# Two-layer mixer and expert network on one core: the delta layer's beta and decay products with the weights standing

## The chip, the cores and the metric

The kernel runs on one core of a Trainium2 chip. The metric is the device time of one execution in microseconds. Engines are named as in the profile: PE is TensorE's matmul, PEld its weight load, DVE is VectorE, ACT ScalarE, POOL GpSimd, and SP the engine that issues most of the DMAs. Everything is in fp32. The program is one launch of 25,742 instructions.

## What is computed

A block of two layers with experts, then a second block of two layers, on 256 tokens of 1024 features. The change is in the odd layer of the first block, the gated delta rule. Cut to what matters:

```python
def gated_deltanet_mixer(h, w_in, conv_w, a_log, dt_bias, o_norm, w_out):
    proj = h @ w_in                                   # 256 tokens x (4096 + 16)
    qkv = silu(causal_dwconv(proj[..., :3072], conv_w))
    q, k, v = split(qkv)
    gate, b_raw, a_raw = split(proj[..., 3072:], (1024, 8, 8))
    q, k = l2norm(q), l2norm(k)
    beta = sigmoid(b_raw)                             # 8 heads
    g = -exp(a_log) * softplus(a_raw + dt_bias)       # 8 heads, the decay
    o = gated_delta_chunked(q, k, v, g, beta)
    return (gated_rmsnorm(o, gate, o_norm)) @ w_out
```

`b_raw` and `a_raw` are the last 16 columns of `h @ w_in`: a product of 256 tokens by 1024 features with 1024 by 16 weights. This is the product that is changed.

## The kernel before

Each engine has one program, written out in order: `res_*` (residual and layer norm), `delta_*` (the delta layer), `moe_*` (experts). Engines meet through counted semaphores: `P.up(...)` marks an event of PE, `V.up` of DVE, `C.up` of ACT, and `e.wait_ge(*on(...))` waits for one. Nothing reorders the work; each engine does its list from top to bottom.

`hT` holds the normed activations with the features on the partitions: eight groups `k` of 128 features, 256 tokens each. A `mm(out, lhsT, rhs)` (line 339 and 340) loads `lhsT` as the standing weights and streams `rhs`; each call in fp32 shows in the trace as two LDWEIGHTS and two MATMUL, so the counts of the trace are twice the calls. A row "128*32 128x256" is a product with standing weights of 128 partitions by 32 columns and 256 streamed columns.

The layer's projection goes in 16 units of 256 columns. Unit 0 is split: `first_unit_pe(e, 0, ...)` does its first 128 tokens between the two halves of the layer norm, with `hT` standing where the second half of the tokens isn't there yet, and the call in `delta_pe` (L1999) does `m = 1`, the other 128 tokens. Each of its four parts is four calls: parts 0 and 1 are output columns 0 to 127, parts 2 and 3 the others. Then `proj_t(e, ("d_ba",), 16, hT, ("d_bac",))` (L2000, the helper at L403) makes the beta and decay columns: for each half `m` of the tokens and each `k`, a 128x128 block of `hT` stands and the 16 columns of the weights stream: 16 calls. Its output lies with tokens on the partitions, in columns 0 to 15 and 256 to 271 of a PSUM bank.

Then PE goes on with `unit_pe(1)`, `unit_pe(2)` (32 calls in all, 256 columns streamed), `sums()` (running sums of the decay, which wait for DVE's event `d_g`), `differences(0)` and `(1)` (64x64 products of `d_gm`), and units 3 to 15, with sums of heads, turns and the sums for the modulation (`ada_sum_pe`, four products with 32 columns of weights into the four quarters of a bank, L589) between them.

DVE's list `delta_dve` begins with the wait for `d_ba` (L2278), copies the 32 columns out of the bank (L2279, event `d_bac`), and works out beta and the decay from them in about twenty small steps up to `d_g`, sixteen `masked` products (`d_gm`), and then the convolution units; after unit 0 of these it waits for `d_cum` 3, the last of PE's `sums()`. ACT's list `delta_act` begins with the wait for `d_bac` (L2182), and copies unit 0 out of its bank (`copy_in(0)`) only behind the exponentials of beta and decay. SP's list `delta_sp` loads unit 0, `d_ba` (64 KB), and then units 1 to 15 into a ring of four slots. A slot is loaded again when PE has used it (`P.also("used", ...)`). POOL loads the modulation's weights in the same way, each released by DVE. The table `tab` of small constants comes in one DMA at the start.

`rs_t` is a tile of 128 by 2 by 512 that holds gate rows for the expert layer before, and decay rows later in the delta layer.

Of the kernel before, what the change touches and what calls it, by code (L numbers as in the profile page):

```python
# [252 lines left out]
def build(nc, A, out, at, lo, tab_at):  # L253
    ctx = ExitStack()
    with ctx:
# [55 lines left out]
        conv_w, colv, hyf = F("conv"), F("cols"), F("hyf")  # L311
        rpe33, gkw2, poolw = F("rpe")[0:33, :], F("gkw2")[0:16, :], F("poolw", 2, 64)
        hw1, hw2, rtb, adt = F("hw1")[0:33, :], F("hw2")[0:64, :], F("rtb", 2, 64), F("adt", 2, 8)
        one_f, sel_f = F("one"), F("sel")
        ident, flip, ones = K("ident"), K("flip"), K("ones")
        eps5, eps6 = K("eps")[:, 0:1], K("eps")[:, 1:2]
        one_c = K("eps")[:, 2:3]
# [18 lines left out]
        def pair(v):  # L336
            return v.rearrange("p (m n) -> p m n", m=2)
# [1634 lines left out]
        def first_unit_pe(e, m, parts=(0, 1, 2, 3)):  # L1972

            u = unit(("d_proj", 0), 8, 256)
            if m == 0 and 0 in parts:
                fill_bank(e, ("d_proj", 0), ("d_raw", 0))
                e.wait_ge(*on("landed", ("d_proj", 0)))
            p = bank("d_proj", 0)
            for part in parts:
                c = part // 2  # L1980
                for k in range(4 * (part % 2), 4 * (part % 2) + 4):
                    if c == 0 and k % 4 == 0:
                        e.wait_ge(*on("n_h", "m0", m, k // 4))
                    t = mm(e, p[:, c * 256 + m * 128:c * 256 + m * 128 + 128], u[:, k, c * 128:c * 128 + 128],
                           hT[:, k, m * 128:m * 128 + 128], k == 0, k == 7, True)
            if m == 1:
                t.then_inc(*P.up("d_proj", 0))
                P.also("used", ("d_proj", 0))

# [6 lines left out]

        def delta_pe(e):
            banks.i = 2
            first_unit_pe(e, 1)  # L1999
            proj_t(e, ("d_ba",), 16, hT, ("d_bac",))  # L2000
            def unit_pe(n):
                proj_f(e, ("d_proj", n), 256, hT, ("d_raw", n))

# [269 lines left out]
        def delta_dve(e):  # L2273
            def chain(i):
                i.then_inc(*V.up("dve"))
                e.wait_ge(*V.now)

            e.wait_ge(*on("d_ba"))  # L2278
            e.tensor_copy(d_ba, pair(bank("d_ba")[:, :])[:, :, 0:16]).then_inc(*V.up("d_bac"))  # L2279
            e.wait_ge(*V.now)  # L2280
            e.tensor_tensor(d_g, d_ba[:, :, 8:16], bc(adt[:, 1, :], 2), ALU.add).then_inc(*V.up("d_gz"))
            e.wait_ge(*on("d_ebe"))
# [1002 lines left out]
def small_table(v):  # L3285

    fields = {}

    def put(name, a):
        a = np.asarray(a, np.float32)  # L3290
        f = np.zeros((128, a.shape[1]), np.float32)
        f[0:a.shape[0]] = a
        fields[name] = f

    def by_feature(a):
        return np.moveaxis(a.reshape(-1, 128, 8), 1, 0).reshape(128, -1)

    def by_column(a):
        return a.reshape(-1, 128).T

    put("cond", by_feature(np.concatenate([v["c"].reshape(1, -1), v["c_2"].reshape(1, -1),
                                           v["c_ctx_2"].reshape(1, -1)])))
    put("modb", by_feature(np.concatenate([v["ada_b"].reshape(12, 1024), v["b_mod_2"].reshape(6, 1024)])))
    put("vec", by_feature(np.concatenate([v["ln_mix_g"], v["ln_mix_b"], v["ln_ffn_g"], v["ln_ffn_b"], v["norm_g_2"],
                                          v["final_g_2"].reshape(1, -1)])))
    put("conv", by_column(v["od_conv_w"][0]))
    cols, n = [], 0
    for name, a in (("hcw", v["hy_conv_w_2"][0]), ("hcb", v["hy_conv_b_2"][0]), ("skip", v["hy_skip_2"][0]),
                    ("psc", v["pool_scale_2"][0]), ("evn", v["ev_norm"]), ("odn", v["od_norm"]),
                    ("qn", v["q_norm_g_2"]), ("kn", v["k_norm_g_2"]), ("gkb", v["ev_gk_b"][0])):  # L3310
        COLS[name] = n
        cols.append(by_column(a))
        n += cols[-1].shape[1]
    put("cols", np.concatenate(cols, 1))
    put("hyf", np.tile(np.concatenate([v["hy_b1_2"], v["hy_b2_2"], v["hy_freq_2"]]).T, (2, 1)))
    put("rpe", np.concatenate([v["rpe_bias"], np.full((1, 4), -1e30, np.float32)]))
    put("gkw2", v["ev_gk_w2"][0])
    put("poolw", v["pool_w_2"][0].reshape(2, 128, 64).transpose(1, 0, 2).reshape(128, 128))
    put("hw1", v["hy_w1_2"][0])
    put("hw2", v["hy_w2_2"][0])  # L3320
    put("rtb", np.broadcast_to(v["moe_router_b"].reshape(1, 128), (128, 128)))
    put("adt", np.broadcast_to(np.concatenate([v["od_a_log"], v["od_dt_bias"]], 1), (128, 16)))
    put("one", np.ones((128, 1)))
    sel = np.zeros((128, 2))
    sel[0:64:32, 0] = 1.0
    sel[64:128:32, 1] = 1.0
    put("sel", sel)
    at, n = {}, 0
    for name, a in fields.items():
        at[name] = (n, a.shape[1])  # L3330
        n += a.shape[1]
    return np.concatenate(list(fields.values()), 1), at


def packed(v):

    out = {}

    def columns(w, a, b):

        return w.reshape(128, 8, -1, 256)[:, :, a // 256:b // 256].transpose(2, 0, 1, 3).reshape(-1, 128, 2048)

    def rows(w):

        return w.reshape(-1, 2, 128, 128, 8).transpose(0, 2, 1, 4, 3).reshape(-1, 128, 2048)

    def sections(w):

        w = w.reshape(-1, 128, 4, 2, w.shape[-1] // 1024, 128, 8)
        return w.transpose(0, 4, 2, 1, 3, 6, 5).reshape(-1, 4, 128, 2048)  # L3350

    out["xT"] = v["x"][0].T.reshape(128, 2048)
    out["ctxT"] = v["ctx_2"][0].T.reshape(128, 2048)
    out["ada"] = np.concatenate([sections(v["ada_w"]), sections(v["w_mod_2"])])
    ev = v["ev_w_in"][0]
    out["ev_in"] = columns(ev[:, 0:3072], 0, 3072)
    out["ev_glr"] = ev[:, 3072:3088].reshape(128, 128)
    od = v["od_w_in"][0]
    out["od_in"] = columns(od[:, 0:4096], 0, 4096)
    out["od_ba"] = od[:, 4096:4112].reshape(128, 128)  # L3360
    out["ev_in2"] = columns(v["ev_w_in_2"][0], 0, 2560)
    out["od_in2"] = columns(v["od_w_in_2"][0], 0, 3584)
    for name, w in (("ev_out", "ev_w_out"), ("od_out", "od_w_out"), ("ev_out2", "ev_w_out_2"),
                    ("od_out2", "od_w_out_2")):
        out[name] = rows(v[w][0])
    out["fn_w"] = v["fn_w_2"][0].reshape(2, 128, 256).transpose(1, 0, 2).reshape(128, 512)
    out["router"] = v["moe_router_w"].reshape(2, 128, 512)
    out["sh_gu"] = np.stack([v["sh_w_gate"], v["sh_w_up"]], 1).reshape(2, 2, 128, 2048)
    out["sh_d"] = rows(v["sh_w_down"]).reshape(2, 128, 2, 8, 128).transpose(0, 3, 1, 2, 4).reshape(2, 8, 128, 256)
    gu = np.stack([v["moe_w_gate"], v["moe_w_up"]], 3).reshape(2, 64, 128, 2, 2048)  # L3370
    out["moe_gu"] = gu.transpose(0, 3, 1, 2, 4).reshape(2, 2, 64 * 128, 2048)
    out["moe_d"] = rows(v["moe_w_down"]).reshape(2, 64 * 128, 2048)
    out["hy_w3_2"] = v["hy_w3_2"][0].reshape(64, 2, 2, 768).transpose(2, 0, 1, 3).reshape(128, 1536)
    return out
# [21 lines left out]
```

## Time and profile before

| | |
|---|---|
| median of 3 executions | 1824.11 us (1821.39 to 1825.58) |
| the profiled execution | 1831.18 us, its span 1829.4 us |
| PE busy | 1750.8 us (96% of the span) |
| PEld busy | 1097.8 us (60%) |
| DVE busy | 756.2 us (41%) |
| ACT busy | 307.4 us (17%) |
| mean DMA rate | 315 GB/s |
| mean granted TensorE clock | 0.983 of full speed |

The expert layers take two long stretches, in which the DMA rate stands at 425 GB/s (about 180 to 640 us and 970 to 1420 us from the start). The delta layer lies between them: its layer norm starts at 675 us, its own list at 685, its last product is at 946. The granted clock is either full (1.00, 2.4 GHz) or half (0.50, 1.2 GHz); a value between is a mean over a stretch that has both.

### The profile page before, as it was taken

The page shows a single profiled execution, that of the slowest core. Times are in us where ns is not written, and L with a number is a line of the kernel's source. Part 1 is how long each engine was busy: PE and PEld are TensorE (multiplying, and loading weights), DVE is VectorE, ACT ScalarE, POOL GpSimd, SP SyncE. Part 2 cuts the span into 40 slices and gives each one's busy share as a digit, 9 for nine tenths or more (in the row PEclk, how much of TensorE's full clock was granted, in tenths as well). Part 3 has the DMA queues.
Part 4 walks back from the last instruction along what each step waited for, and adds up shares of the span by engine and source line. Part 5 has one row for each costly group of instructions (what it writes and reads, how often), then busy time and mean ns, then how long its engine had stood idle before and what let it go on. Part 6 is the DMA issues. An engine that isn't in the chain of part 4 may idle for free.

```text
span 1829.4 us, 25742 instructions
## 1 busy us (share of the span) xinstructions
PE 1750.8 (96%) x10440; PEld 1097.8 (60%) x10440; DVE 756.2 (41%) x1545; ACT 307.4 (17%) x667; POOL 45.7 (2%) x86
## 2 busy tenths in 40 slices
PE   7999999999999899998999999999999899999998
PEld 3886645454444348788856454444443487778874
DVE  2557522222222136878864222222211457564173
ACT  1111401000000022341232010000000222220121
POOL 0100000000000000000000000000000000000000
PEclk9989999999999999999899999999999899999999
DMA  9967699999999986774467999999999775135301
GB/s 403 386 262 313 284 385 425 424 424 425 424 425 425 426 346 235 286 254 172 184 277 322 392 425 424 424 425 425 425 425 425 299 278 196 52 113 188 120 29 40
DMA packets 82094, 576.81 MB, mean 315 GB/s; under 512 B 9132, under 2 KB 11436, under 8 KB 12848
## 3 DMA queue, kind: packets, MB, share of 16 engines
q1 hardware_dynamic: 70992, 494.65, 65.7%
q0 software_dynamic: 10976, 80.43, 11.4%
q8 instruction: 86, 1.41, 0.3%
q14 instruction: 40, 0.33, 0.0%
HBM read 573.98 MB, written 1.06 MB: 314 GB/s over the span
## 4 chain that ended last, share of the span: by engine, by line
PE 63%; DMA 20%; SPq 11%; DVE 3%; issue 1%; ACT 0%; DVEq 0%; ACTq 0%
PE ps L340 61%; SPq L1484 10%; DMA slab<-in_moe_gu 8%; DMA wbuf<-in_moe_gu 7%; DMA wbuf<-in_ev_in 2%; PE ps L344 2%; DMA cst<-in_moe_gu 1%; DMA hma<-in_moe_gu 1%; SPq L1500 1%; DVE hma L563 1%; DVE gds L754 0%; DMA wbuf<-in_ada 0%; SPq L1495 0%; DVE slab L3164 0%; DVE slab L3161 0%
## 5 line engine op out<-in xcount | busy, mean ns | idle before, releaser
L340 PE MATMUL ps<-slab 128*128 128x128 f32 (+10 forms) x3240 | 571.6, 361 | 18.2 <-DMA slab<-in_moe_gu 15.7
L340 PEld LDWEIGHTS ps<-slab 128*128 128x128 f32 (+4 forms) x3240 | 349.7, 171 | 200.3 <-issue 160.3
L340 PE MATMUL ps<-hma,wbuf 128*128 128x256 f32 (+2 forms) x1552 | 341.1, 380 | 2.3 <-DMA wbuf<-in_ev_in 1.7
L340 PE MATMUL ps<-wbuf,slab 128*32 128x512 f32 (+3 forms) x1176 | 321.0, 600 | 14.5 <-DMA wbuf<-in_moe_gu 14.1
L340 PEld LDWEIGHTS ps<-hma,wbuf 128*128 128x128 f32 (+1 forms) x1552 | 290.7, 192 | 48.7 <-issue 5.5
L347 ACT ACTIVATE slab<-ps 128x256 f32<-128x256 f32 (+4 forms) x119 | 54.3, 470 | 882.5 <-PE ps L340 870.5
L340 PEld LDWEIGHTS ps<-wbuf,slab 128*32 128x32 f32 (+2 forms) x1176 | 102.0, 134 | 157.3 <-issue 126.6
L1736 DVE TENSOR_TENSOR slab<-ps,slab 128x256 f32<-128x256 f32 x44 | 18.7, 425 | 383.5 <-ACT slab L347 383.5
L340 PE MATMUL ps<-hma,slab 128*32 128x512 f32 (+2 forms) x440 | 170.9, 557 | 2.5 <-DMA hma<-in_moe_gu 2.5
L563 DVE SCALAR_TENSOR_TENSOR hma<-wbuf,cs,hma 128x1024 f32<-128x1024 f32 x102 | 130.8, 1282 | 10.4 <-DMA wbuf<-in_ada 6.8
L340 PE MATMUL ps<-slab,cst 128*32 128x512 f32 (+7 forms) x422 | 111.0, 535 | 5.3 <-ACT slab L347 5.3
L340 PE MATMUL ps<-cst,slab 128*32 128x512 f32 (+6 forms) x452 | 113.0, 447 | 2.1 <-DMA cst<-in_moe_gu 2.1
L340 PE MATMUL ps<-wbuf,cst 128*64 128x512 f32 (+1 forms) x376 | 111.3, 596 | 2.2 <-DMA wbuf<-in_moe_gu 2.2
L1764 DVE TENSOR_TENSOR slab<-ps,rs_t 128x512 f32<-128x512 f32 x88 | 60.9, 692 | 75.0 <-PE ps L340 75.0
L340 PE MATMUL ps<-wP,slab 64*64 64x64 f32 (+2 forms) x400 | 78.7, 366 | 4.9 <-DMA wP<-in_moe_gu 3.6
L1751 DVE COPY slab<-ps 128x512 f32<-128x512 f32 x44 | 30.4, 692 | 119.3 <-PE ps L344 119.2
L340 PEld LDWEIGHTS ps<-hma,slab 128*32 128x32 f32 (+2 forms) x440 | 53.9, 136 | 43.0 <-issue 33.1
L340 PEld LDWEIGHTS ps<-slab,cst 128*32 128x32 f32 (+4 forms) x422 | 44.0, 147 | 35.6 <-issue 32.0
L340 PE MATMUL ps<-hma,cst 128*32 128x256 f32 (+3 forms) x272 | 62.5, 475 | 0.3 <-DMA hma<-in_moe_gu 0.3
L340 PEld LDWEIGHTS ps<-wbuf,cst 128*64 128x64 f32 (+1 forms) x376 | 31.3, 131 | 51.3 <-issue 44.0
L347 ACT ACTIVATE hma<-ps 128x512 f32<-128x512 f32 (+1 forms) x41 | 20.6, 504 | 224.3 <-PE ps L340 224.3
L344 PE MATMUL ps<-cst,slab 128*128 128x128 f32 x368 | 52.6, 278 | 5.8 <-DVE slab L352 5.5
(282 smaller groups left out, 1479.3 us busy)
## 6 DMA issues: line engine op xcount, KB each, us to landing
wbuf<-in_moe_gu SPq DMA_DIRECT2D x91, 1024.0 KB, 24.5
slab<-in_moe_gu SPq DMA_DIRECT2D x75, 1024.0 KB, 23.7
wbuf<-in_moe_d SPq DMA_DIRECT2D x75, 1024.0 KB, 26.2
wbuf<-in_ada POOLq DMA_DIRECT2D x60, 1024.0 KB, 6.5
hma<-in_moe_gu SPq DMA_DIRECT2D x43, 1024.0 KB, 24.1
cst<-in_moe_gu SPq DMA_DIRECT2D x36, 1024.0 KB, 19.7
wbuf<-in_od_in SPq DMA_DIRECT2D x30, 1024.0 KB, 4.9
wbuf<-in_ev_in SPq DMA_DIRECT2D x22, 1024.0 KB, 9.4
```

The costliest lines, as they stand in the source:

```text
L340: return e.matmul(o, lhsT, rhs, start=start, stop=stop, skip_group_check=skip)
L344: return e.transpose(o, i, ident[0:n, 0:n])
L347: return e.activation(o, i, fn, bias=bias, scale=scale, accum_out=acc)
L563: t = e.scalar_tensor_tensor(total, w, cs[:, c, k:k + 1], total, ALU.mult, ALU.add)
L1484: e.dma_start(place(s)[:, 0:src.shape[1]], src).then_inc(*Q.arrive(f"w{s}", key))
L1500: [e.value_load(order[0:1, l, x:x + 1], min_val=0, max_val=128 * (NE - 1)) for x in range(p0, p0 + n)])]
L1736: e.tensor_tensor(m_hh[:, q % 2, :], bank("m_gu", l, q)[:, 256:512], m_sg[:, q % 2, :], ALU.mult).then_inc(*V.up("m_hh", l, q))
L1751: e.tensor_copy(m_tp[:, q % 2, :], bank("m_tt", l, q)[:, :]).then_inc(*V.up("m_ttc", l, q))
L1764: e.tensor_tensor(m_ys[:, q % 2, f * 512:f * 512 + 512], bank("m_ys", l, q, f)[:, :], g_rows[f], ALU.mult).then_inc(*V.up("m_ysc", l, q, f))
```

## The change

The 16-column product is turned round. In place of `hT` standing, the weights of one group of 128 features stand (16 columns, filled with zeros to 32) and all 256 tokens of `hT` stream. The eight groups go to four column tiles: group `k` writes the 32 partitions from `32 * (k % 4)`, so each quarter of the bank adds up two of the eight groups: 8 calls. The bank then holds, in each quarter, a partial sum with the 16 outputs on the partitions. DVE copies these 128 by 256 values to `rs_t`, and two calls with the copied block standing and a constant `sum4` (128 by 16: four identities one below the other) streaming add the four quarters up and turn the result, so that tokens are on the partitions again. They go to columns 256 to 287 of the same bank. DVE's copy to `d_ba` follows as before.

In PE's list the eight calls stand between parts 0, 1 and parts 2, 3 of unit 0's second half; the two turning calls stand behind part 3 and wait for DVE's copy. Event `d_proj` 0 and its "used" come after part 3, which is later in the list than before by the eight calls. The slot of `d_ba` is given back after the eight calls. `od_ba` in memory grows from 64 to 128 KB, `tab` by 16 columns.

```diff
-        one_f, sel_f = F("one"), F("sel")
+        one_f, sel_f, sum4 = F("one"), F("sel"), F("sum4")
...
-            if m == 1:
+            if m == 1 and 3 in parts:
                 t.then_inc(*P.up("d_proj", 0))
                 P.also("used", ("d_proj", 0))
...
         def delta_pe(e):
             banks.i = 2
-            first_unit_pe(e, 1)
-            proj_t(e, ("d_ba",), 16, hT, ("d_bac",))
+            first_unit_pe(e, 1, (0, 1))
+            u = unit(("d_ba",), 8, 32)
+            p = fill_bank(e, ("d_ba",), ("d_bac",))
+            e.wait_ge(*on("landed", ("d_ba",)))
+            for k in range(8):
+                r = 32 * (k % 4)
+                t = mm(e, p[r:r + 32, 0:256], u[:, k, :], hT[:, k, :], k < 4, k > 3, True)
+            t.then_inc(*P.up("d_bag"))
+            P.also("used", ("d_ba",))
+            first_unit_pe(e, 1, (2, 3))
+            e.wait_ge(*on("d_bagc"))
+            for m in range(2):
+                t = mm(e, p[:, 256 + 16 * m:272 + 16 * m], rs_t[:, 0, m * 128:m * 128 + 128], sum4, True, True)
+            t.then_inc(*P.up("d_ba"))
...
+            e.wait_ge(*on("d_bag"))
+            e.tensor_copy(rs_t[:, 0, 0:256], bank("d_ba")[:, 0:256]).then_inc(*V.up("d_bagc"))
             e.wait_ge(*on("d_ba"))
-            e.tensor_copy(d_ba, pair(bank("d_ba")[:, :])[:, :, 0:16]).then_inc(*V.up("d_bac"))
+            e.tensor_copy(d_ba, pair(bank("d_ba")[:, 256:288])).then_inc(*V.up("d_bac"))
...
+    put("sum4", np.tile(np.eye(32, 16), (4, 1)))
...
-    out["od_ba"] = od[:, 4096:4112].reshape(128, 128)
+    out["od_ba"] = np.pad(od[:, 4096:4112].reshape(128, 8, 16), ((0, 0), (0, 0), (0, 16))).reshape(128, 256)
```

## Rows read from the trace of the kernel before

**Rows 1.** The page's slices: busy tenths, granted clock and DMA rate in 40 slices.
```profile
PE   7999999999999899998999999999999899999998
DVE  2557522222222136878864222222211457564173
PEclk9989999999999999999899999999999899999999
```
**Rows 2.** Timeline of PE, 676 to 697 us: start, us, instructions, count.
```profile
682.83 6.42 PE L340 MATMUL ps<-hma,wbuf 128*128 128x128 f32 x56
689.08 4.56 PE L340 MATMUL ps<-wbuf,hma 128*128 128x16 f32 x32
```
**Rows 3.** Timeline of PE, 693 to 860 us, same columns; in brackets the idle time before.
```profile
693.48 16.49 PE L340 MATMUL ps<-hma,wbuf 128*128 128x256 f32 x64
709.81 2.16 PE L340 MATMUL ps<-gds,cst 128*128 128x8 f32 x16
711.90 2.08 PE L340 MATMUL ps<-cst,slab 64*64 64x64 f32 x64
713.91 27.89 PE L340 MATMUL ps<-hma,wbuf 128*128 128x256 f32 x128
741.64 3.60 PE L340 MATMUL ps<-slab,cst 128*128 128x512 f32 x8
745.17 0.64 PE L340 MATMUL ps<-hma,cst 128*32 128x256 f32 x8
745.74 14.08 PE L340 MATMUL ps<-hma,wbuf 128*128 128x256 f32 x64
...
831.72 3.53 PE L340 MATMUL ps<-cst,wP 64*64 64x64 f32 x64 [2.45 <-DVE wP L2382]
```
**Rows 4.** Stretches of line 340: us, PE and PEld busy (count), granted clock, DMA share, GB/s.
```profile
689.08:691.56 2.48, 2.48 (x25) 2.48 (x24) 1.00 0.92 330
691.56:693.48 1.92, 1.92 (x11) 1.92 (x11) 0.51 0.98 397
693.48:698.38 4.90, 4.90 (x13) 3.91 (x14) 0.50 0.67 231
698.38:709.80 11.42, 11.42 (x54) 10.06 (x53) 1.00 0.25 92
```
**Rows 5.** Stretches, all engines: PE, PEld, DVE, ACT, POOL busy, clock, DMA share, GB/s.
```profile
708.60:712.10 3.50, 3.44 (x29) 3.15 (x29) 0.09 (x1) 0.00 (x0) 0.00 (x0) 1.00 0.32 63
831.50:835.00 3.50, 3.28 (x62) 3.31 (x64) 2.54 (x5) 2.45 (x3) 0.00 (x0) 0.51 0.79 332
```
**Rows 6.** Groups of the whole run by form: busy us, mean ns of one, idle before.
```profile
L340 PE MATMUL ps<-hma,cst 128*32 128x256 f32 x144 | 11.5, 391 | 0.0
L3134 DVE COPY wP<-ps 128x256 f32<-128x256 f32 x12 | 4.2, 416 | 10.0 <-PE ps L344 10.0
```
**Rows 7.** Timeline of DVE, 693 to 800 us.
```profile
693.68 0.19 DVE L2279 COPY gds<-ps 128x32 f32<-128x32 f32 x1 [9.73 <-PE ps L340]
...
698.21 2.69 DVE L351 TENSOR_SCALAR slab<-cst,gds 128x64 f32<-128x64 f32 x16
...
712.01 0.17 DVE L2332 COPY gds<-ps 128x16 f32<-128x16 f32 x1 [7.83 <-PE ps L340]
```
**Rows 8.** Timeline of ACT, 684 to 713 us.
```profile
684.42 5.69 ACT L347 ACTIVATE xT<-ps,comb 128x128 f32<-128x128 f32 x16
```
**Rows 9.** SP's loads of od_in, issues at 675.2 and 689.3 us, to landing.
```profile
L382 SPq DMA_DIRECT2D wbuf<-in_od_in x1: 652/652/652, 675.2 to 675.2; - x1
DMA to landing us min/median/max: 11.7/11.7/11.7
...
L382 SPq DMA_DIRECT2D wbuf<-in_od_in x1: 328/328/328, 689.3 to 689.3; - x1
DMA to landing us min/median/max: 6.1/6.1/6.1
```
**Rows 10.** The chain of waits, from 660 us: start, us, what.
```profile
682.99 28.32 PE ps L340 x164
711.32 0.04 issue
711.36 48.46 PE ps L340 x276
```
**Rows 11.** The chain of waits, from 870 us.
```profile
934.78 6.45 DMA wbuf<-in_ada
...
1081.54 23.94 DMA hma<-in_moe_gu
```
**Rows 12.** SP's waits, 660 to 1010 us: total, times, longest.
```profile
SPq L1500 <- DVE order L1337: 19.2, 1, 19.2
```

## The prediction

> **What bounds the kernel now.** I read the slices of the page first [rows 1]: PE is busy nearly everywhere, DVE only in the delta layer (slices 15 to 20) and near the end, and the granted clock dips a little in a few slices. So the question is whether the edited place lies on the path that sets the end. The chain of waits answers it: from 682.99 us on it is PE alone, 28.32 us and, after 0.04 us of issue, another 48.46 us [rows 10], and the whole delta layer until 829 us has no idle PE. The product that changes stands in this chain: 32 matmuls from 689.08 to the next start at 693.48, 4.40 us [rows 2, 3]. The granted clock is the second thing to see. It was full until 691.56 us, 2.48 us after the 16-column products began, and then half (0.51, 0.50) until 698.38, full again behind that [rows 4]. Half of this low stretch lies under the two units that follow, which nobody edits.
>
> **What the old product costs.** Its own time is 4.40 us. At the full clock it would be shorter: the 56 matmuls before it, with the same 128 standing columns, start every (689.08 - 682.83) / 56 = 0.112 us [rows 2], so 32 take 3.58 us, and 0.82 us is the slow clock's. The two units behind it take 709.81 - 693.48 = 16.33 us for 64 matmuls. The same form at the full clock starts every (741.64 - 713.91) / 128 = 0.2166 us, 64 of them in 13.86 [rows 3]. So the low clock costs another 2.47 us there. Old cost in this execution: 4.40 + 2.47 = 6.87 us; without any dip 3.58.
>
> **What the new product costs.** (a) Eight calls, 16 matmuls of 128*32 by 256 columns on four column tiles. The modulation's sums are this form, on four column tiles too: eight of them from 745.17 to 745.74, 0.57 us, and they begin 3.53 us after eight 512-column products that at 2 x 0.2166 each take 3.47, so 0.06 more on entering [rows 3]. If four tiles run at once, eight stream 2 x 0.2166 = 0.43 us, and the rest, 0.14 + 0.06 = 0.20, is for changing form there and back. Sixteen: 0.87 + 0.20 = 1.07 us. What that row doesn't show is two products after each other into the same quarter; if that broke the overlap, each would cost its whole 0.391 us [rows 6], 16 x 0.391 = 6.26 us, the upper end; I take 1.07, since the row is of the same form.
> (b) Two turning calls, four matmuls with 128 standing columns: 4 x 0.112 = 0.45 us.
> (c) The wait for DVE's copy. Behind the eight calls PE has parts 2 and 3, 16 matmuls x 0.112 = 1.79 us. The path to be covered is the last product's 0.39, a copy of 128x256 from PSUM, 0.42 [rows 6], and some 0.2 for the two handovers (DVE began at 693.68, 0.20 after PE's next start [rows 2, 7]): about 1.0 us. Cover 1.79, so nothing; without the cover it would be 1.0. DVE is idle for 9.73 us before `d_ba` [rows 7], so the copy displaces nothing, and behind PE's waiting instruction all the units are queued, which is what a miss would hold up.
> (d) Parts 2 and 3 are only moved. Event `d_proj` 0 comes 1.07 us later, at 690.2 instead of 689.1. Who waits for it: ACT's copy, which stands behind beta's exponentials anyway and so comes earlier, and SP's load of unit 3, issued at 689.3 and landed 6.1 later [rows 9]. Landed at 696.5 it is still more than 7 us ahead of unit 3's turn (713.91 less the gain). Nothing.
> (e) The loads: 64 KB more for `d_ba` just ahead of unit 1's. At the 425 GB/s of the loaded stretches this is 0.15 us. Unit 2's load, issued at 675.2, landed after 11.7 us at 686.9, unit 1's before it [rows 9]; PE will want unit 1 at about 690.7 instead of 693.5. Margin of over 3 us, nothing. `tab` grows by 8 KB at the start: 0.02 us.
> (f) ACT must be free when `d_bac` comes: its copies to `xT` end at 690.11 [rows 8], the new `d_bac` comes at about 691. Nothing, but only 0.8 us of room.
>
> PE reaches unit 1 after 1.07 + 0.45 = 1.52 us of new work. **Sum:** 3.58 - 1.52 = 2.06 us without any regard to the clock; 6.87 - 1.52 = 5.35 us if the dip goes altogether.
>
> **Does the clock stay up?** What the engine did before the fall was 2.48 us of products with 16 columns streamed [rows 4]. In the same trace 2.09 us of even thinner ones (8 columns, `sums()`, 709.81 to 711.90) left the clock at 1.00, and the 64x64 products behind them too [rows 3, 5]. The new form has 0.45 us of thin products in one piece and 1.07 us of column tiles that stream 256 columns, apart from it by 1.8 us of full ones. So I expect no fall here. But `sums()` and `differences` follow earlier than they did, and other places of the kernel will meet the chip's watch on activity at other moments.
> The Trainium skill, TensorE: Matmul & The Clock Gate, in its closing table of what matters, says that keeping TensorE busy continuously gets it to full clock, and keeping out idle gaps holds it there. PE was busy for all 1.92 us of 691.56 to 693.48 at a clock of 0.51 and had no gap before. The row disagrees with the rule read by busy time; by the rule the dip has another cause and would stay, which is the second case below.
> The skill's TensorEngine Tiling, section PSUM Bottleneck, speaks against this change: tiling makes TensorE faster but not the emptying of PSUM, and the copy may become the bound. Here the copy is extra work, some 1.0 us with its handovers; by the rule the gain would be smaller by this, by the rows it is covered by 1.79 us of parts 2 and 3.
>
> **How much of it reaches the end.** DVE: its chain starts with `d_ba`, and runs through `d_g` and the 16 masked products (ended 700.9) to a wait of 7.83 us for PE at 712.01 [rows 7]. PE gains 2.47 us on it in between, leaving 5.4: DVE doesn't become the bound, and its convolutions begin earlier by the whole gain. From there on PE and DVE hold the same distance. The next PE wait, 2.45 us at 831.72 for DVE [rows 3], hangs on PE's own products before it. Behind, the modulation's load waited for at 934.78 (6.45 us) [rows 11] is issued when DVE frees a slot, so it moves along. In the expert layer SP waits 19.2 us for the order of the experts [rows 12], which comes from the layer norm; the loads of the chain (1081.54, 23.94 us [rows 11]) start from there. So the DMA-bound stretch moves as a whole, and nothing in it has a date of its own. I count the gain at the end as the gain in PE's list.
>
> **From the profiled execution to the median.** The profiled execution took 1831.18 us, 7.1 over the median. Its after would be 1831.18 - 5.35 = 1825.8. But 5.35 has the dip at the length it had in this one execution, 6.8 us at half clock. Where PE waited for DVE, the dip at 831.5 to 835.0 has half that length [rows 5]; a dip like this would cost 3.4 / 2 = 1.7 us and the gain would be 2.06 + 1.7 = 3.8. Whether the timed executions have the long or the short one isn't shown. I take the middle of 3.8 and 5.35, 4.5: 1824.11 - 4.5 = 1819.6 us, own range of this case 1817.5 to 1821.5.
>
> **The rivals.**
> 1. The dip stays, or comes back nearby (under `sums()` and `differences`, which now come sooner after the turning). For: 0.51 of clock at full busy shows that it isn't idleness. Against: the thin work falls from 4.40 us to 0.45 in a piece. Gain 2.06 us: 1822.0.
> 2. The gain is made in the delta layer and not seen at the end: half-clock stretches further on (after PE's waits at 831 us and in the layer norms) fall otherwise than before and take back some 3.4 us of half clock, 1.7 us each, twice. 4.5 - 3.4 = 1.1: 1823.0. For: such stretches are in the trace, and the executions of before lie 4.2 us apart. Against: they can as well fall away.
> 3. Slower: products into the same column tile don't overlap. It decides at the start of group 4, which adds to what group 0 wrote, and if PE waits for each product to end, 16 x 0.391 + 0.20 + 0.45 = 6.91 us stand in place of 4.40. The clock's dip then stays too: loss of 2.5 us, 1826.6. Against: the modulation's eight in 0.57 us, which at two matmuls per call already add into one place. It is neutral up to 0.25 us a product (4.40 - 0.65 over 15).
> 4. The change doesn't do what it says: the wait for `d_bagc` isn't covered, 1.0 us of PE standing still, perhaps with a fall of the clock. Gain 4.5 - 1.0 = 3.5: 1820.6, within the range.
>
> **Chances.** Forecast (with rival 4 as its upper part) 0.62; rival 1 0.20; rival 2 0.12; slower 0.06, of which half is beyond 0.2%. A measurement of this kernel can tell about 0.2% from no change, 3.65 us. Of the forecast's 0.62 the part under 3.65 us (1820.5 and up) is a good fifth, 0.14; rivals 1 and 2 are within 0.2% save for noise of a microsecond, which throws about 0.05 over the line. Faster 0.52, same 0.45, slower 0.03. The range for 8 in 10 goes from the long dip with one more stretch at half clock gone further on (1824.1 - 5.35 - 1.7 = 1817.0) to rival 2's and the measurement's own scatter of a microsecond, 1824.0.
>
> **What the profile after would show.** 16 matmuls 128*32 by 256 columns at about 687.3 us that take 1.1 us to the next start (6 would be rival 3); DVE's new copy ending before part 3 does; four matmuls with 16 columns right behind part 3, with no idle before; `d_ba`'s copy at about 690.9 instead of 693.7; clock 1.00 between 687 and 710 and 64 matmuls in 13.9 us (else rival 1); PE's `sums()` at about 704.5. The distance from `sums()` to the first idle PE (831.7 before) should be unchanged, and so should that to the end; if it grows, rival 2. I would be wrong altogether if DVE's wait of 7.83 us were gone, or if PE waited for unit 1's landing.

## The result

The changed kernel takes 1839.37 us (median of 4 executions, 1837.28 to 1842.66) against 1824.84 (4, 1821.39 to 1826.89): a ratio of 1.0076, with a 95% interval of 1.0047 to 1.0104. It is slower, where 1819.6 was forecast and 1817 to 1824 given as the range. The profiled execution took 1842.66 us; that of the kernel before, 1831.18, lay some 6 us above its own median, so the two traces are 11.5 us apart and the medians 14.5.

The page of the changed kernel, its span, granted clock and DMA rate in 40 slices:

```profile
span 1840.9 us, 25719 instructions
PEclk9989999999999999999899999999999899999999
GB/s 398 378 256 313 284 384 421 421 420 420 419 420 420 422 341 274 295 258 142 179 276 321 417 422 421 420 420 420 420 421 421 286 284 187 61 91 192 121 26 45
```

and the rate of the kernel before, in the same 40 slices:

```profile
GB/s 403 386 262 313 284 385 425 424 424 425 424 425 425 426 346 235 286 254 172 184 277 322 392 425 424 424 425 425 425 425 425 299 278 196 52 113 188 120 29 40
```

The row of the clock, in tenths, is the same as before [rows 1], but its mean is not: 0.975 of full speed where it was 0.983, and 0.975 to 0.980 in the four executions. As the clock is either full or half, 0.975 means about 2 x 0.025 x 1840.9 = 92 us at half clock and 0.983 about 62 (estimates from the means). This comes back further down. The rate of the loads differs too: in the expert stretches 424 to 426 GB/s have become 419 to 422, already from slice 7 on, 400 us before the delta layer begins. In two stretches of 300 us, one from each expert layer (us, PE, PEld, DVE, ACT and POOL busy, clock, DMA share, GB/s), first before and then after:

```profile
300.00:600.00 300.00, 286.16 (x1685) 138.65 (x1684) 66.98 (x150) 26.40 (x70) 0.00 (x0) 0.99 1.01 425
1050.00:1350.00 300.00, 286.81 (x1698) 138.61 (x1692) 67.00 (x150) 26.40 (x70) 0.00 (x0) 0.99 1.01 425
```

```profile
300.00:600.00 300.00, 285.39 (x1664) 136.35 (x1664) 65.44 (x147) 25.61 (x68) 0.00 (x0) 0.98 1.01 420
1050.00:1350.00 300.00, 285.62 (x1680) 137.72 (x1676) 65.06 (x147) 26.47 (x70) 0.00 (x0) 0.98 1.01 420
```

The packets of 8192 bytes that carry the expert weights took 310.5 ns each on average from 290 to 590 us before, and 314.3 after. In the edited place all went as forecast. PE's timeline after (start, us, count), which answers [rows 2, 3]:

```profile
689.58 7.61 PE L340 MATMUL ps<-hma,wbuf 128*128 128x128 f32 x72
697.03 0.52 PE L340 MATMUL ps<-tab,rs_t 128*128 128x16 f32 x4
697.40 14.06 PE L340 MATMUL ps<-hma,wbuf 128*128 128x256 f32 x64
711.29 2.16 PE L340 MATMUL ps<-gds,cst 128*128 128x8 f32 x16
713.38 2.08 PE L340 MATMUL ps<-cst,slab 64*64 64x64 f32 x64
```

The 72 matmuls at 689.58 are the 24 and 32 of unit 0 and the 16 new ones among them, merged. From 682.83 to 709.81 it was 26.98 us before; from 689.58 to 711.29 it is 21.71. The stretch gained 5.27 us, and came 6.75 us late.

Two places show how the lateness adds up. The cast of the experts' order (L1337, one in each expert layer) and the layer norms' L777 (three), with the first and the last start, before and after:

```profile
L1337 DVE CAST order<-ps x2: 212/212/212, 208.1 to 966.3; 1x64 int32<-1x64 f32 x2
L777 DVE TENSOR_TENSOR comb<-tab,mods x3: 157/159/161, 178.4 to 944.1; 128x8 f32<-128x8 f32 x3
```

```profile
L1337 DVE CAST order<-ps x2: 213/214/214, 210.3 to 969.5; 1x64 int32<-1x64 f32 x2
L777 DVE TENSOR_TENSOR comb<-tab,mods x3: 158/159/160, 180.6 to 947.3; 128x8 f32<-128x8 f32 x3
```

So in this pair of executions: +2.2 us before the first experts' order (208.1 to 210.3), +4.55 in the first expert layer (to the 6.75 above), -5.27 in the changed stretch, +1.7 in the rest of the delta layer (944.1 to 947.3 is +3.2 in all), +4.4 in the second expert layer (its layer norm's statistics start at 1434.51 and 1442.09), and +3.9 in the second block, of which 3.4 are a fall of the clock at 1643 us that the execution before didn't have. The span is 11.5 us longer. The 4.55 and 4.4 us are the rate's: they are the same in both expert layers, and 1.2% of some 400 us is about as much. The others go with the clock where I looked: from 38 to 50 us it was 0.86 on average after and 1.00 before, which is 1.7 us, and in the delta layer behind the change (715 to 946 us) 0.96 against 0.97.

### The profile page after: what moved, and what is told of

It reads as the page before. It is cut to its first block, busy times and chain, and to the rows that moved or that the text cites. A ratio compares the mean times of both kernels' runs of the same rounds, so it can differ in the third digit from the quotient of the medians.

```text
span 1840.9 us, 25719 instructions
## 1 busy us (share of the span) xinstructions
PE 1760.1 (96%) x10428; PEld 1101.7 (60%) x10428; DVE 756.3 (41%) x1546; ACT 307.8 (17%) x667; POOL 45.8 (2%) x86
## 3 DMA queue, kind: packets, MB, share of 16 engines
q0 software_dynamic: 10976, 80.43, 11.5%
## 4 chain that ended last, share of the span: by engine, by line
PE 63%; DMA 19%; SPq 13%; DVE 3%; issue 2%; ACT 0%; DVEq 0%; ACTq 0%
PE ps L340 61%; SPq L1484 11%; DMA slab<-in_moe_gu 8%; DMA wbuf<-in_moe_gu 4%; DMA wbuf<-in_ev_in 2%; PE ps L344 2%; DMA cst<-in_moe_gu 1%; DMA wP<-in_moe_gu 1%; DMA hma<-in_moe_gu 1%; SPq L1500 1%; DVE hma L563 1%; DVE gds L754 0%; DMA wbuf<-in_ada 0%; SPq L1495 0%; DVE slab L3179 0%
## 5 line engine op out<-in xcount | busy, mean ns | idle before, releaser
L340 PE MATMUL ps<-slab 128*128 128x128 f32 (+10 forms) x3240 | 584.7, 369 | 17.8 <-DMA slab<-in_moe_gu 15.3
L340 PEld LDWEIGHTS ps<-slab 128*128 128x128 f32 (+4 forms) x3240 | 356.6, 173 | 201.7 <-issue 161.2
L340 PE MATMUL ps<-hma,wbuf 128*128 128x256 f32 (+3 forms) x1568 | 344.5, 382 | 2.4 <-DMA wbuf<-in_ev_in 1.7
L340 PEld LDWEIGHTS ps<-hma,wbuf 128*128 128x128 f32 (+2 forms) x1568 | 292.8, 192 | 50.1 <-issue 6.0
L340 PE MATMUL ps<-hma,slab 128*32 128x512 f32 (+2 forms) x440 | 176.6, 572 | 3.3 <-DMA hma<-in_moe_gu 3.2
```

What stands on the lines that cost most here:

```text
L340: return e.matmul(o, lhsT, rhs, start=start, stop=stop, skip_group_check=skip)
```

## The experiments

Kernels whose names begin with x are the kernel before with an edit, those with y the changed kernel with one. "Place" is where a tile begins in a partition of SBUF, worked out from the order and sizes of the allocations (wbuf 57,344 bytes, cst 34,584, tab 4,440 before and 4,504 after, then xT, hma, slab, small tiles, wP). Each was timed beside executions of the kernel before, on five chips in all, where its medians are 1826.5 to 1827.2. Where no number is given, a median is of 8 to 12 executions.

**Which of the edits slows the loads.** The diff touches the rate by nothing that it computes. It widens the table by 16 columns and od_ba by 64 KB.

x_table:
```diff
+    put("sum4", np.tile(np.eye(32, 16), (4, 1)))
```


> The kernel before with one edit: the constant field sum4 is appended to the small table, which nobody reads. The table grows by 16 columns (64 bytes in a partition, 8 KB in memory), and every tile that is allocated behind tab in SBUF (xT, hma, slab, rs_t, wP and the rest) moves by 64 bytes; wbuf and cst do not. Not a single instruction of the delta layer differs. In the changed kernel the DMA rate in both expert stretches is 420 GB/s where it was 425, which costs 4.4 us in each, and all of it lies in code that the diff does not touch. Theory A (moved tiles behind tab, or the table's size in memory): slow, rate 420, +9 to +19 us over before (there is no gain of the delta layer here, so it should be slower than the changed kernel by up to 5 us). Theory B (the size of od_ba in memory shifts the expert weights): no change, 1824 +- 2. Theory C (the new products or the different order of the work do it): no change.

Measured: 1836.11 (9 executions) to 1826.76, 1.0049 (1.0034 to 1.0064); 420 GB/s in both stretches. 9.4 us for a constant that isn't used.

x_odba:
```diff
-    out["od_ba"] = od[:, 4096:4112].reshape(128, 128)
+    out["od_ba"] = np.pad(od[:, 4096:4112].reshape(128, 8, 16), ((0, 0), (0, 0), (0, 16))).reshape(128, 256)
...
-            u = unit(key, 8, n)
+            u = unit(key, 8, 32)[:, :, 0:n] if key == ("d_ba",) else unit(key, 8, n)
```


> The kernel before with one edit: od_ba is padded to 128 KB in memory and loaded whole, the old 16 products read every 32nd-column block of it. SBUF addresses as before; whatever lies behind od_ba in memory may lie 64 KB further. Theory A (table): no change, 1824 +- 2, rate 425. Theory B (od_ba's size in memory): rate 420 and +9 to +19 us. Theory C (the new work): no change.

Measured: 1823.77, 0.9983 (0.9967 to 0.9999); 425 GB/s. Theory B falls. I can't explain the 3.0 us below before. PE's work is the old one, and yet the interval doesn't reach 1; so a difference of this size can turn up without new work, and the next kernel, timed beside the same executions of before, has to be read with this in mind.

y_tile_last:
```diff
-        tab = sb("tab", [128, A["table"].shape[1]])
+        tw = A["table"].shape[1] - 16
+        tab = sb("tab", [128, tw])
...
         wP = sb("wP", [128, 16, 128])
+        sum4 = sb("s4", [128, 16])
...
+            e.dma_start(sum4[:, :], A["table"][:, tw:tw + 16]).then_inc(*Q.arrive("in_s4", "s4"))
```


> The changed kernel with the tile of sum4 allocated last in SBUF, loaded by a DMA of its own (8 KB) behind that of d_ba; tab has its old width, so all tiles lie where they were in the kernel before. The table in memory is still 8 KB larger, od_ba still 128 KB. Theory A in its SBUF form: rate 425 again, and the delta layer's gain shows: 1819 to 1821. Theory A in its memory form, and theory B: rate 420, 1839 as the changed kernel. Theory C (new work): 1839.

Measured: 1823.10, 0.9981 (0.9964 to 0.9998); 425 GB/s. The same new products, the same larger arrays, and the loss is gone. The median is 3.7 us below before, where 1819 to 1821 was expected, and x_odba had 3.0 of this without the new products.

y_odba_small, with `u` of 8 by 16 and od_ba as it was:
```diff
-                t = mm(e, p[r:r + 32, 0:256], u[:, k, :], hT[:, k, :], k < 4, k > 3, True)
+                t = mm(e, p[r:r + 16, 0:256], u[:, k, :], hT[:, k, :], k < 4, k > 3, True)
```


> The changed kernel with od_ba left at 64 KB: the eight products have 16 standing columns instead of 32 and write 16 of each 32 partitions of the bank; the turning product meets old contents of the other partitions with zeros. The table is wider as in the change. Theory A (table, either form): 1839, rate 420. Theory B: rate 425 and 1819 to 1821. Theory C: 1839.

Measured: 1832.86, 1.0030 (1.0015 to 1.0045); 420 GB/s. Slow, so A, but 6.5 us under the 1839 that was expected. I come back to that.

**The place, or the table's longer rows.** 

x_hole64:
```diff
         tab = sb("tab", [128, A["table"].shape[1]])
+        sb("hole", [128, 16])
```


> The kernel before with 64 unused bytes in each partition allocated behind tab. Nothing is loaded into them; the table, every DMA's size and every instruction are those of before; xT, hma, slab, rs_t, wP and all tiles behind lie 64 bytes further, wbuf and cst where they were. Theory A1 (the place of the tiles): as the kernel with the wider table, 1836 +- 3, DMA rate 420 and 314 ns for a packet of 8192 bytes in the expert stretches. Theory A2 (the longer rows of the table's own load, or its size in memory): as before, 1826, rate 425, 310.5 ns.

Measured: 1835.25, 1.0047 (1.0030 to 1.0065). Its two stretches:

```profile
300.00:600.00 300.00, 283.98 (x1654) 136.59 (x1647) 65.32 (x146) 26.46 (x70) 0.00 (x0) 0.99 1.01 420
1050.00:1350.00 300.00, 284.59 (x1680) 137.56 (x1674) 66.99 (x150) 26.46 (x70) 0.00 (x0) 0.99 1.01 420
```

420 GB/s again. Not one instruction and not one byte of traffic differs from the kernel before; 64 bytes are left free behind tab, and 8 us are lost. Theory A2 falls; the place of the tiles behind tab is the cause.

**What in the place.** Ten kernels move it by other amounts; the diffs are the line above with another width, or in another position.

y_hole64, `sb("hole", [128, 16])` in the changed kernel:

> The changed kernel, whole, with the same 64 unused bytes behind its wider tab: the tiles lie 128 bytes further than before the change, so their place within 128 bytes is the old one (slab at 112 modulo 128), within 256 not (240 instead of 112). Theory A1 with a period of 128 bytes: 1823, rate 425. Theory A1 with a longer period, or with any move as the cause: 1836 to 1839, rate 420. Theory A2: 1839.

Measured: 1832.57, 1.0031 (1.0014 to 1.0049), 420 GB/s.

y_align256, `sb("hole", [128, 20])` in the changed kernel:

> The changed kernel with 80 unused bytes behind tab: xT, hma and slab begin at a multiple of 256 bytes (112 modulo 256 before the change, 176 in the changed kernel), the small tiles behind them and wP shift with them (wP 24 modulo 128). If a write is dear where it starts off a boundary, this is at least as fast as the old place: 1823 or less, rate 425 or more. If it is a matter of how far the tiles lie from wbuf and cst or from each other, it can be either. Theory A2: 1839.

Measured: 1832.98, 1.0030 (1.0012 to 1.0049), 420 GB/s. A multiple of 256 bytes is slow.

x_hole_late, the 64 bytes behind slab:

> The kernel before with 64 unused bytes behind slab instead of behind tab: xT, hma and slab stay, only the small tiles (mods, rs_t, gds and others) and wP lie 64 bytes further. If the large tiles that the weights are loaded to (hma, slab) are what matters: rate 425, packets of 310.5 ns, 1827. If the small tiles or wP are: rate 420, 314 ns, 1835.

Measured: 1827.03, 0.9999 (0.9985 to 1.0014), 425 GB/s. Moving the small tiles and wP by 64 bytes costs nothing.

x_hole_first, the 64 bytes ahead of wbuf:

> The kernel before with 64 unused bytes ahead of wbuf: every tile lies 64 bytes further and none moves against another. If the distance between tiles matters (wbuf and cst against hma and slab): rate 425, 1827. If the place itself matters: slow, rate 420 or lower, since now wbuf and cst are off their multiples of 256 bytes too, 1835 or more.

Measured: 1834.02, 1.0045 (1.0026 to 1.0063), 420 GB/s. The distance between tiles isn't the thing by itself.

x_hole512, `sb("hole", [128, 128])`:

> The kernel before with 512 unused bytes behind tab: xT, hma and slab keep their place within 512 bytes (112). A pattern with a period of 512 bytes or less: rate 425, 1827, which 64, 128 and 144 bytes did not give. If any move behind tab is dear: rate 420, 1835.

Measured: 1827.97, 1.0001 (0.9985 to 1.0018):

```profile
300.00:600.00 300.00, 286.07 (x1678) 138.34 (x1672) 66.54 (x150) 26.46 (x70) 0.00 (x0) 1.00 1.01 425
1050.00:1350.00 300.00, 287.61 (x1688) 138.45 (x1687) 66.98 (x150) 26.07 (x70) 0.00 (x0) 0.99 1.01 425
```

x_hole16, `sb("hole", [128, 4])`:

> The kernel before with 16 unused bytes behind tab: slab at 128 modulo 256. The smallest move. If the old place was one lucky one among many: rate 420, 1835. If a rate of 425 is had by most places and 64, 128 and 144 bytes were unlucky: 1827.

Measured: 1840.50 (4 executions), 1.0084 (1.0058 to 1.0111), 420 GB/s.

x_hole256, `sb("hole", [128, 64])`:

> The kernel before with 256 unused bytes behind tab: xT, hma and slab at 368 modulo 512, the same place as before within 256. If the pattern's period is 256 bytes: rate 425, 1827. If it is 512: rate 420, 1835.

Measured: 1828.69, 1.0011 (0.9993 to 1.0029), 425 GB/s.

x_hole448, `sb("hole", [128, 112])`:

> The kernel before with 448 unused bytes behind tab: xT, hma and slab at 48 modulo 512. Slow places so far are 128, 176, 240 and 256. If the fast places are the first quarter of each 512 bytes: rate 425, 1827. If 112 alone is fast: 420, 1835.

Measured: 1832.92, 1.0036 (1.0018 to 1.0055), 421 GB/s.

y_align512, `sb("hole", [128, 84])` in the changed kernel:

> The changed kernel with 336 unused bytes behind tab: xT, hma and slab begin at a multiple of 512 bytes. The multiple of 256 that was tried was 256 modulo 512 and slow. If a boundary of 512 is the rule (112 being near enough to it): rate 425 or better, 1823 or less. If 112 is a lucky place of its own: 420, 1833.

Measured: 1833.99, 1.0040 (1.0024 to 1.0057), 420 GB/s. With hma and slab moved together and wbuf left alone, moves of 0, 256 and 512 bytes, which keep the place at 112 modulo 256, have 425 GB/s; the five other places modulo 256 (0, 48, 128, 176, 240) have 420 or 421.

y_hole448, `sb("hole", [128, 112])` in the changed kernel, which brings hma and slab to 512 bytes behind the old place:

> The changed kernel, whole, with 448 unused bytes behind its wider tab, so that xT, hma and slab lie 512 bytes further than before the change, at 112 modulo 512 as there. If the period of 512 holds and the place explains all of the loss: rate 425, 1822 to 1824, that is 3 to 5 us below before, as with the constant's tile put last. If the new work has a cost of its own elsewhere: above 1827.

Measured: 1823.64 (12 executions) to 1827.15, 0.9978 (0.9961 to 0.9995):

```profile
300.00:600.00 300.00, 286.10 (x1688) 139.42 (x1687) 66.53 (x150) 25.68 (x69) 0.00 (x0) 0.99 1.01 425
1050.00:1350.00 300.00, 286.74 (x1681) 137.20 (x1680) 66.51 (x149) 26.47 (x70) 0.00 (x0) 0.99 1.01 425
```

The change, whole, is 3.5 us under the kernel before once its tiles lie well, and some 15 us under the changed kernel. How firm are the 3.5 us? The kernels with the old product in its old order and 425 GB/s lie at -3.0 (x_odba), +0.5 (x_hole_late), +1.5 (x_hole512) and +1.5 (x_hole256) beside before, the two with the change and 425 GB/s at -3.7 and -3.5. Among the kernels at 420 or 421 GB/s, x_hole16 apart, those with the change lie at +5.4 to +6.8 and those without at +5.8 to +9.4. All of it points to a gain of 2 to 4 us, but no single comparison is far outside what x_odba shows without one.

**Which tile, and whether there is a rule.**

x_slab_only, the 64 bytes between hma and slab:

> The kernel before with 64 unused bytes between hma and slab: only slab (176 modulo 256) and the small tiles behind move, which alone cost nothing; xT and hma stay at 112. If slab's loads are what matters: rate 420 or a little above, 1833 to 1835. If it is xT or hma (hT, the operand of many products, is in it): rate 425, 1827.

Measured: 1836.03, 1.0046 (1.0029 to 1.0062), a time like the slow kernels', but a rate between the two:

```profile
300.00:600.00 300.00, 286.07 (x1660) 136.62 (x1653) 65.46 (x146) 26.41 (x70) 0.00 (x0) 0.99 1.01 422
1050.00:1350.00 300.00, 285.51 (x1688) 137.44 (x1684) 66.06 (x149) 26.41 (x70) 0.00 (x0) 0.99 1.01 422
```

y_all112:
```diff
+        sb("hole1", [128, 28])
         wbuf = sb("wbuf", [128, 7, 2048])
+        sb("hole2", [128, 58])
         cst = sb("cst", [128, A["consts"].shape[1]])
         tab = sb("tab", [128, A["table"].shape[1]])
+        sb("hole3", [128, 26])
...
+        sb("hole4", [128, 58])
         wP = sb("wP", [128, 16, 128])
```


> The changed kernel with unused bytes ahead of wbuf, cst, xT and wP (112, 232, 104, 232), so that every tile that expert weights are loaded to begins at 112 modulo 256: wbuf (0 before), the loaded part of cst (24 before), hma and slab (112 before, 176 in the changed kernel), wP (136 before). If 112 modulo 256 is good for any target of a load: packets at 309 to 310 ns everywhere, rate 426 or 427, and the time 2 to 4 us below the 1823.6 of the changed kernel with hma and slab put back. If the fast state needs the mixture that there was (wbuf at 0): rate 420, 1833.

Measured: 1824.92, 0.9992 (0.9979 to 1.0004), 423 and 424 GB/s:

```profile
300.00:600.00 300.00, 286.79 (x1680) 138.25 (x1672) 65.92 (x148) 26.40 (x70) 0.00 (x0) 0.99 1.01 423
1050.00:1350.00 300.00, 286.07 (x1674) 136.03 (x1673) 66.26 (x149) 26.40 (x70) 0.00 (x0) 0.99 1.01 424
```

Neither of the two expectations. Its packets to wbuf went down from 311 ns to 310, but those to slab, at the same place modulo 256 as before, went up from 309.7 to 314. So 112 isn't good in itself; the places of several tiles act together. Slab alone, moved, costs 3 GB/s of the 5, and slows the packets to wbuf too (311 to 313), which hasn't moved. What goes on in the chip stays open.

That the rate costs what it seems to cost can be read from all twenty profiles. Take the time from the first L1337 to the start of PE's long row of unit 0 (208.1 to 682.83 us before), which is nearly the whole first expert layer. It is 474.7 to 475.1 us in the eight kernels with 425 GB/s, 475.7 with 423 and 424 (y_all112), 477.7 with 422 (x_slab_only), 478.5 with 421 (x_hole448), and 479.0 to 479.6 in the nine with 420. So the lower rate costs 4.3 us or a little more in this layer, with and without the new product, and as much again in the second: some 9 us. The longer time of x_slab_only is then not the rate's alone; its executions had a mean granted clock of 0.982, those of before beside them 0.986.

**The clock under the old product.**

x_split:
```diff
-            first_unit_pe(e, 1)
-            proj_t(e, ("d_ba",), 16, hT, ("d_bac",))
+            first_unit_pe(e, 1, (0, 1))
...
+            for m in range(2):
+                if m:
+                    first_unit_pe(e, 1, (2, 3))
+                for k in range(8):
+                    i = mm(e, p[:, m * 256:m * 256 + 16], hT[:, k, m * 128:(m + 1) * 128], u[:, k, :], k == 0, k == 7)
```


> The kernel before with its old sixteen 16-column products in two halves, with parts 2 and 3 of unit 0 between them; no product is added or taken away, all tiles lie where they lay. Theory of the clock (a long piece of thin products makes the granted clock fall, and the fall costs up to 2.5 us under units 1 and 2): each half is 1.8 us of thin products, the clock stays at 1.00 from 686 to 710 us, the 64 matmuls of units 1 and 2 take 13.9 us instead of 16.3, and the time is 0 to 3 us below before. Rival (the clock falls for another reason): units 1 and 2 at 16.3 us as before, time as before. DMA rate 425 by both.

Measured: 1824.09 to 1827.14, 0.9987 (0.9969 to 1.0005), so the time alone is unclear. Its timeline of PE:

```profile
684.16 1.86 PE L340 MATMUL ps<-wbuf,hma 128*128 128x16 f32 x16
687.74 1.86 PE L340 MATMUL ps<-wbuf,hma 128*128 128x16 f32 x16
689.44 14.06 PE L340 MATMUL ps<-hma,wbuf 128*128 128x256 f32 x64
```

The next row starts at 703.34: 13.90 us for the 64 matmuls, no fall. But the kernels with the undivided product show that one such timeline isn't enough. x_hole512, and then x_hole64, the same instructions:

```profile
686.10 3.64 PE L341 MATMUL ps<-wbuf,hma 128*128 128x16 f32 x32
689.60 14.06 PE L341 MATMUL ps<-hma,wbuf 128*128 128x256 f32 x64
```

```profile
690.37 3.64 PE L341 MATMUL ps<-wbuf,hma 128*128 128x16 f32 x32
693.86 15.75 PE L341 MATMUL ps<-hma,wbuf 128*128 128x256 f32 x64
```

From the start of the old product to the start of `sums()` it is 17.39 us in x_hole512 and x_hole_late, 19.07 in x_table, x_hole16, x_hole64, x_hole_first and x_hole448, and 20.73 in the kernel before, x_odba, x_hole256 and x_slab_only. One piece of code has three prices: no fall of the clock, a short one, and the long one that the trace before happened to show. The mean of the eleven is (2 x 17.39 + 5 x 19.07 + 4 x 20.73) / 11 = 19.37 us.

## Why the prediction was wrong

**What bounds the kernel, and the price of the new work: right.** The new product and its changes of form took 7.45 - 56 x 0.112 = 1.2 us (7.45 from 689.58 to 697.03; 1.07 forecast), the turning 697.03 to 697.40, 0.37 (0.45), the units behind them 13.89 (13.86). The four column tiles overlap, with the second four adding onto the first; their row after, of the form that [rows 6] priced:

```profile
L340 PE MATMUL ps<-hma,wbuf 128*32 128x256 f32 x16 | 1.1, 385 | 0.0
```

Sixteen in 1.1 us, each 385 ns long: rival 3 would have had them in 6.3. The gain of this stretch in the pair of profiled executions, 5.27 us, is the 5.35 of the sum.

**The wait for DVE's copy: right.** DVE's new copy and then `d_ba`'s, with the idle time ahead of them, where it was one wait of 9.73 us [rows 7]:

```profile
695.28 0.42 DVE L2292 COPY rs_t<-ps 128x256 f32<-128x256 f32 x1 [4.59 <-PE ps L340]
697.59 0.19 DVE L2294 COPY gds<-ps 128x32 f32<-128x32 f32 x1 [1.88 <-PE ps L340]
```

It ends at 695.70, and the turning starts at 697.03, right behind part 3. The rule of the Trainium skill (TensorEngine Tiling, PSUM Bottleneck) that the emptying of PSUM may become the bound doesn't bite here: 0.42 us of copy stand under 1.8 us of other products.

**The clock under the new work: right where it was looked for, too large as a term.** Units 1 and 2 ran at full clock, `sums()` and `differences` too (line 340):

```profile
697.40:711.20 13.80, 13.80 (x66) 12.17 (x66) 1.00 0.63 234
711.29:715.40 4.11, 4.05 (x82) 3.85 (x80) 1.00 0.70 229
```

All eight profiles of the new form have 13.89 us there. By the rule that I set against the row (the Trainium skill, TensorE: Matmul & The Clock Gate, the closing table), busy time keeps the clock up; PE had no gap there [rows 4], and yet the clock fell, at this place, in nine of the eleven profiles with the undivided old product and in none of the nine without it (x_split and the eight of the new form). That bears out the row. But rival 1 holds too, one place further on. In y_hole64 the clock fell behind `sums()`:

```profile
708.00:713.00 5.00, 4.94 (x31) 4.44 (x29) 0.00 (x0) 0.00 (x0) 0.00 (x0) 1.00 0.23 64
713.00:720.00 7.00, 7.00 (x82) 6.31 (x82) 6.48 (x13) 4.00 (x8) 0.53 (x1) 0.76 0.67 260
```

From the start of `sums()` to the next heads' product (the eight of 128x512) it is 33.40 us there and 31.83 in y_hole448 and in the changed kernel itself: 1.57 us. It did so in four of the eight profiles of the new form (y_odba_small, y_hole64, y_align256, y_all112), at 713 to 716 us in three and at about 706 in the other. With this the expected gain is 19.37 - (1.57 + 13.89) - 4/8 x 1.57 = 3.1 us, not 4.5, and y_hole448 and y_tile_last measured 3.5 and 3.7 in medians. So one term was mis-sized, by some 1.4 us: I took the middle between a long and a half fall (3.8 and 5.35), when none at all was a third case, and I took rival 1 for an outcome of its own, when it is 1.57 us lost in half of the profiles. A smaller slip: I wrote that half of the low stretch lies under the next two units; by [rows 4] it is 4.90 of 6.82 us.

The same thing elsewhere is the +3.4 us of the second block. Behind 24 products that stream one column:

```profile
1640.49 3.09 PE L340 MATMUL ps<-cst 128*128 128x1 f32 x24
1643.44 11.88 PE L340 MATMUL ps<-hma,wbuf 128*128 128x256 f32 x40
```

the clock was 0.77 on average from 1640 to 1655 us after. Before, the same 24 start at 1632.20, and it was 1.00 there:

```profile
1640.00:1655.00 15.00, 15.00 (x66) 12.80 (x65) 7.26 (x16) 1.20 (x2) 0.00 (x0) 0.77 0.06 8
```

```profile
1630.00:1645.00 15.00, 15.00 (x77) 12.56 (x76) 10.53 (x24) 1.79 (x3) 0.00 (x0) 1.00 0.14 42
```

The code there is the same in both, and the clock fell at it in four of the twenty profiles. A single pair of profiled executions carries several microseconds of this in each direction.

**Where the step failed: "`tab` grows by 8 KB at the start: 0.02 us", and "the DMA-bound stretch moves as a whole".** These two steps made the forecast wrong in its direction. The first priced the bytes of the load and not what the width of a tile does to those that are allocated behind it. The second took 425 GB/s as given. The rate is a condition of 900 us of this kernel, so 1.2% of it is about 10 us, twice all that the edit could bring; no rival named it, and the range was made from terms of the edited stretch alone. x_hole64 shows it without any of the change: 8 us for 64 bytes. y_hole448 has the change without it, and its median is 3.5 us under before.

**Rival 2 came too, on that occasion.** The rate's 9 us less the gain's 3 gives 1831 to 1833, and y_odba_small, which has every tile where the changed kernel has it, and y_hole64 and y_align256 measured 1832.6 to 1833.0. The changed kernel's four executions, at another time, took 1839.4. What tells them apart in the record is the granted clock: it is 0.984 on average in the 30 executions of those three kernels, and 0.978 in the changed kernel's four. Among the 30, an execution whose clock is lower by 0.001 takes 0.9 us more (so it is in the 142 executions of before, too), and at 0.978 their line gives 1839.5; the mean of the four is 1839.7. So the remaining 6 to 7 us go with more half clock spread over the kernel (0.006 lower on average is some 22 us more of it, an estimate from the means), which is rival 2, priced at 3.4 us. Three of those 30 at 0.979 and 0.980 took 1839.3, 1839.0 and 1837.2 us. x_hole16, also from four executions, at 0.975 to 0.979, lies some 5 us over the other slow places, and the low clock accounts for at least a part of it. Why the clock fell oftener in just these fours, and not in those of before beside them (1821.4 to 1826.9 us the first time, a mean clock of 0.987 beside x_hole16), stays open; no run shows that the change does it.

## What to carry to other kernels

Where a kernel streams weights at the limit of its DMA engines, widening any tile moves all that are allocated behind it, and this alone can cost more than the edit gains: keep new constants in a tile of their own at the end of the list, or fill up to the old place modulo 256 bytes, and compare the rate of the long loads before looking at the edited place. A product that streams few columns costs more than its own time, since the clock may fall under what follows; turned round onto column tiles it took 1.6 us, the turning back included, for 3.5 to 4.4. What one profiled execution shows of the clock is one draw of several: count the same stretch in more profiles before it enters a sum at its full size.

## What the runs showed of the hardware that I had not expected

The rate of long loads depends on where their targets begin in SBUF: 425 GB/s with wbuf at 0 and hma and slab at 112 modulo 256 bytes, 420 or 421 with hma and slab at 0, 48, 128, 176 or 240. I have no rule for it: with wbuf and the others at 112 as well it was 423 and 424. The Trainium skill's DMA: Bandwidth & Descriptors, section How a descriptor splits into AXI transactions, says of reads that each transaction starts at a boundary of 256 bytes, and that where a descriptor starts off it, the bytes from the boundary below are fetched too and cost beats. If writes into SBUF followed the same rule, places at 0 would be best; y_align256 and y_align512 had hma and slab there, at 420 GB/s. The measurement decides.

All loads slow down together, also those to tiles that haven't moved, and not at once. In x_hole64, behind the pause of the queue at 207 us and the one at 245, the packets of 8192 bytes took 309 to 310 ns for 8 to 12 us (211 to 219 us the first time), and then mostly 313 to 314 for as long as the stretch lasted; behind the pause at 966 us both lengths alternate for some 15 us first.
